# Three of the last gathers of a Trainium2 kernel split at token 120 into two gathers each

## The chip, the core and the metric

The kernel runs on one core of a Trainium2 chip. The metric is the device time of one execution in microseconds (us). The kernel before takes 1238.28 us, the median of 3 runs (1238.28 to 1238.28).

## The reference

Two blocks are computed on 256 tokens of width 1024 in fp32: a first block with a convolution branch, a differential attention and a cross attention, and a second block with a stick-breaking attention, a recurrent unit and, last, a PEER layer. The change lies in the PEER layer only:

```python
def chunk(xc):                                  # 128 tokens
    q = jnp.einsum('td,dhk->thk', xc, w_query)
    ...
    s = jnp.einsum('thpk,hpnk->thpn', q, sub_keys).astype(jnp.float32)
    top_s, top_i = lax.top_k(s, PEER_TOPK)
    ...
    idx = jnp.take_along_axis(cand_i, best_pos, axis=-1)
    g = jax.nn.softmax(best_s, axis=-1)
    u = jnp.take(expert_u, idx, axis=0)
    v = jnp.take(expert_v, idx, axis=0)
    act = jax.nn.gelu(jnp.einsum('td,thkd->thk', xc, u))
    return jnp.einsum('thk,thkd->td', (g * act).astype(v.dtype), v)
```

Each token picks 16 experts in each of 8 heads, 128 in all, out of 16384. An expert is a row u and a row v of 1024 fp32 numbers each. The token's output is the sum over its picks of a weight, times gelu(x . u), times v.

## The kernel before, in words

Up to about 590 us the kernel computes the first block and the mixing half of the second: weights are loaded piece by piece by SyncE (SP), each is split in two fp32r parts by ScalarE (ACT) and VectorE (DVE), and TensorE (PE) multiplies. From there to the end it works on the PEER layer, which is a loop over 256 picks, numbered g = 0 to 255. The tokens lie in two tiles t of 128, one token on a partition. Head by head and tile by tile (the list heads, 16 entries), each entry has 16 picks: picks 224 to 239 belong to entry 14, picks 240 to 255 to entry 15, both of tile 1.

For a pick g the four engines do this:

- **GpSimd (POOL)**, function gather (L2429 on): it waits until the expert's numbers are chosen ("picked") and until the buffer is free, and then issues one indirect DMA. It fetches for each of 128 tokens the 8 KB of its expert, u and v together, into a buffer of 128 x 2048 fp32 (1 MB). There are nine buffers in a ring (rows, UV): conv_in, three called big, four called row, and work_two. Gather g takes buffer g modulo 9, so it waits for PE to end pick g - 9. Each buffer has a semaphore of its own, gather0 to gather8.
- **DVE**, dot_product (L2062 in the profile): multiplies u with the tokens and sums, so it waits for the gather's semaphore. Then weigh (L2072) makes the coefficient.
- **ACT**, spread_value: the gelu (L1293), and then the coefficient on the diagonal of a 128 x 128 matrix (L1299).
- **PE**, add_value (L779): four matmuls of that diagonal with v, which add up in PSUM.

The order on DVE is dot_product(g + 1), weigh(g), and one step of choosing the experts of a later head: the steps of entry 14 start at pick 198, those of entry 15 at pick 214 (choose_at). Their end, which marks "picked", is L2034.

The last two picks, 254 and 255, are HALVED: u and v come by separate gathers of half rows (gather_half, L2440 on), both u first, then both v. The last v is not multiplied on PE but added by DVE (last_value, L2080); add_values (L2091) then adds PSUM to the residual, and SP and ACT write the halves of the output, SP at L2505, ACT at L1574. Tile 0's output is written earlier, some picks after pick 223.

SP has no work between its last weight load, at 577 us, and the output of tile 0.

The core of gather, which the change touches:

```python
e.indirect_dma_start(
    out=UV.ap(g), out_offset=None, in_=experts,
    in_offset=bass.IndirectOffsetOnAxis(ap=expert[t][:, n:n + 1], axis=0)
    ).then_inc(*mark(f"gather{g % len(rows)}", None, ("row", g), by=16))
```

Of the kernel before, what the change touches and what calls it, by code (L numbers as in the profile page):

```python
# [7 lines left out]
P = 128  # L8
F32 = mybir.dt.float32
F32R = mybir.dt.float32r  # L10
U32 = mybir.dt.uint32
# [29 lines left out]
PEER_TOPK = 16  # L41
# [21 lines left out]
class Marks:  # L63
# [13 lines left out]
    def mark(self, kind, key=None, *others, by=1):  # L77

        value = self.values[kind] = self.values.get(kind, 0) + by
        for name in (("#" + kind, value), (kind, key), *others):  # L80
            self.names[name] = kind, value
        return self.sem(kind), by
# [108 lines left out]
def build(nc, known, x, mem, vectors, weights, rg_w_a, rg_w_x, norm_ffn, sub_keys_t, experts,  # L191
          out):
    with ExitStack() as ctx:
        def sb(name, shape, dt=F32, space=ctx):
            return space.enter_context(nc.sbuf_tensor(name, [P, *shape], dt))

        def psum(name, n):
# [3 lines left out]
        mark, now, at = marks.mark, marks.now, marks.at  # L201
# [15 lines left out]
        ident, ones, ones64, later = (sb(n, [P]) for n in (  # L217
            "ident", "ones", "ones64", "later"))
# [1 line left out]
        ident_r, mask_r = (sb(n, [P], F32R) for n in ("ident_r", "mask_r"))  # L220
        iota16 = sb("iota16", [PEER_TOPK])
        col = sb("col", [144])
        sb("rows to 512 bytes", [96])

        def split_pair(space, name, columns):
            return [sb(f"{name}_{part}", [KT, columns], F32R, space) for part in ("hi", "lo")]
# [19 lines left out]
        def flat(ap):  # L246
            return ap.rearrange("p k t -> p (k t)")
# [79 lines left out]
        expert = [sel[:, t * 128:(t + 1) * 128].bitcast(U32) for t in range(TT)]  # L327
# [45 lines left out]
        for p in range(PIECES_ALL):  # L373
# [7 lines left out]
        rows = [sb(f"row{i}", [2 * D])[:, :] for i in range(4)]  # L381
        rows = [flat(conv_in[:, :, :])[:, 0:2 * D], big[2][:, :], big[0][:, :], big[1][:, :],
                *rows[2:], *rows[:2], work_two[:, :]]
# [4 lines left out]
        UV = Ring("uv", rows)  # L388
        diag_places = [probs.buffers[i % 2][:, i // 2 % 2, i // 4 * P:(i // 4 + 1) * P]
                       for i in range(12)]  # L390
        heads = [(t, h) for i in range(4) for t in range(TT) for h in (2 * i, 2 * i + 1)]
# [5 lines left out]
        for g in range(ALL_PICKS):  # L397
            UV.take(g)
        HALVED = (ALL_PICKS - 2, ALL_PICKS - 1)
        LAST = ALL_PICKS - 1  # L400
        final_sum = {t: max(g for g in range(LAST) if picks[g][0] == t) for t in range(TT)}
        half_rows = experts.rearrange("n (h d) -> (n h) d", h=2)
# [15 lines left out]
        def pe(e):  # L418
# [339 lines left out]
            def score(i, tiles=range(TT)):  # L758
                for t in tiles:
                    bank = banks.take(("score", i, t))  # L760
                    for wait in W(("queries", (i, t)), ("keys", None),
                                  banks.free(("score", i, t))):
                        e.wait_ge(*wait)
                    for j in range(4):
                        m = e.matmul(bank[:, j * P:(j + 1) * P],
                                     queries[:, j, t * P:(t + 1) * P], keys[:, 4 * i + j, :],
                                     start=True, stop=True)
                    m.then_inc(*mark("side_scores", (i, t), *([("scored", i)] if t else [])))

            def add_value(g):  # L770
                t, first = picks[g][0], g == first_pick[picks[g][0]]
                if first:
                    units.take(("y", t), t)
                unit = units.ap(("y", t))
                for wait in W(("diag", g), ("row", g) if g in HALVED else None,
                              units.free(("y", t)) if first else None):
                    e.wait_ge(*wait)
                for half in range(2):
                    m = e.matmul(unit[:, half * 512:(half + 1) * 512], diag_places[g % 12],  # L779
                                 UV.ap(g)[:, D + half * 512:D + (half + 1) * 512],  # L780
                                 start=first, stop=g == final_sum[t])
                    if half == 0 and g == final_sum[t]:
                        m.then_inc(*mark("added_half", t))
                m.then_inc(*mark("added", g, ("uv free", g)))
# [89 lines left out]
            score(0, [1])  # L874
            for g in range(LAST):
                add_value(g)
# [15 lines left out]
        def act(e):  # L892
# [394 lines left out]
            def spread_value(g):  # L1287
# [5 lines left out]
                e.activation(here, here, ACT.Gelu_apprx_tanh).then_inc(*mark("gelu", g))  # L1293
                if g == LAST:
                    return
# [283 lines left out]
        def dve(e):  # L1579
# [390 lines left out]
            def choose(head, eights=(0, 1)):  # L1970
# [68 lines left out]
                if head == len(heads) - 1:  # L2039
                    n = len(HALVED)  # L2040
                    e.scalar_tensor_tensor(out=row_f, in0=place_f[0][:, -n:],
# [15 lines left out]
            def dot_product(g):  # L2057
                t, n = picks[g]
                row_u = UV.ap(g)[:, 0:D]
                for wait in W(("row u" if g in HALVED else "row", g), ("h3", t)):  # L2060
                    e.wait_ge(*wait)
# [14 lines left out]
            def last_value():  # L2076
                t, n = picks[LAST]
                for wait in W(("coef", LAST), ("row", LAST)):
                    e.wait_ge(*wait)
                e.scalar_tensor_tensor(out=x_res[:, t, :], in0=UV.ap(LAST)[:, D:2 * D],  # L2080
                                       scalar=coef[t][:, n:n + 1], in1=x_res[:, t, :],
                                       op0=ALU.mult, op1=ALU.add).then_inc(*mark("last value"))
# [311 lines left out]
        def pool(e):  # L2394
            W = Reached(at)
# [33 lines left out]
            def gather(g):  # L2429
                t, n = picks[g]  # L2430
                for wait in W(("picked", g // PEER_TOPK, g % PEER_TOPK // 8),
                              UV.free(g) if g >= len(rows) else ROW_FREE[g]):
                    e.wait_ge(*wait)
                e.indirect_dma_start(  # L2434
                    out=UV.ap(g), out_offset=None, in_=experts,
                    in_offset=bass.IndirectOffsetOnAxis(ap=expert[t][:, n:n + 1], axis=0)
                    ).then_inc(*mark(f"gather{g % len(rows)}", None, ("row", g), by=16))

            def gather_half(g, half):
                i = HALVED.index(g)  # L2440
                for wait in W(("half rows", None), UV.free(g)):
                    e.wait_ge(*wait)
                e.indirect_dma_start(
                    out=UV.ap(g)[:, half * D:(half + 1) * D], out_offset=None, in_=half_rows,
                    in_offset=bass.IndirectOffsetOnAxis(ap=half_row[half][:, i:i + 1], axis=0)
                    ).then_inc(*(mark(f"gather{g % len(rows)}", None, ("row", g), by=16) if half
                                 else mark(f"gather u{i}", None, ("row u", g), by=16)))
# [13 lines left out]
            for c, base in ((slice(0, 256), -P), (slice(256, 384), 0)):  # L2461
                n = c.stop - c.start
# [12 lines left out]
            add_up("mix sB", P)  # L2475
            for g in range(HALVED[0]):
                gather(g)
            for half in range(2):
                for g in HALVED:
                    gather_half(g, half)  # L2480
# [3 lines left out]
        def sp(e):  # L2484
            W = Reached(at)
            for half in range(2):
                c = slice(half * SLOT, (half + 1) * SLOT)
                e.dma_start(x_tm[:, :, c], x_in[:, :, c]).then_inc(
                    *mark(f"load_x{half}", None, ("loaded", "x", half), by=16))
            for p in load_order:  # L2490
                place, prior = raw.place[p], raw.prior[p]
                for wait in W(RAW_FREE[p] if p in RAW_FREE else
                              None if prior is None else ("lo", prior)):
                    e.wait_ge(*wait)
                i = e.dma_start(flat(raw.ap(p)[:, :, :]), weights[p])
                i.then_inc(*mark(f"load_w{place}", p, ("loaded", p), by=16))
                if p == slot["pq0"].pieces[1]:
                    for wait in W(("scan", None)):
                        e.wait_ge(*wait)
                    e.dma_start(ffn_gain, norm_ffn).then_inc(  # L2500
                        *mark("load_gain", None, ("ffn gain", None), by=16))
            for t in range(TT):
                for wait in W(("y_out", (t, 0))):
                    e.wait_ge(*wait)
                e.dma_start(out_tm[:, t, 0:SLOT], x_res[:, t, 0:SLOT]).then_inc(  # L2505
                    *mark(f"out{t}0", by=16))
            for name in ("out00", "out10", "out01", "out11"):
                for wait in W((name, None)):
                    e.wait_ge(*wait)

        with nc.Block() as block:
            block.tensor(pe)
            block.scalar(act)
            block.vector(dve)
            block.gpsimd(pool)
            block.sync(sp)
# [66 lines left out]
```

## Time and profile before

| | us |
|---|---|
| median of 3 runs | 1238.28 |
| the profiled execution | 1239.19 |
| its span, first to last instruction | 1237.0 |
| PE busy | 1097.0 (89%) |
| DVE busy | 979.1 (79%) |
| POOL busy | 590.0 (48%) |
| ACT busy | 549.7 (44%) |

The profiled execution is 0.91 us above the median, and 2.2 us of it lie outside the span. Engine names: PE TensorE, PEld its weight loads, DVE VectorE, ACT ScalarE, POOL GpSimd, SP SyncE; a q behind a name (POOLq, SPq) is the engine's own instruction queue, from which DMAs are issued. A timeline row gives the start in us, the duration in us, the engine, the line, the operation, out<-in, and in brackets the engine's idle time before it and what ended that. In the rows of GB/s a stretch is cut in 40 equal slices. The core has 16 DMA engines, and every digit of a DMA row is their mean busy share in tenths.

### The profile page before, as it was taken

What the parts mean: (1) busy time and instruction counts of PE and PEld (TensorE: products, weight loads), DVE (VectorE), ACT (ScalarE), POOL (GpSimd) and SP (SyncE); (2) the same over time, 40 slices, a digit from 0 to 9 for tenths busy, and PEclk for the clock granted to TensorE, in tenths of its full rate; (3) what the DMA queues carried; (4) which work ended last, traced back from release to release, by engine and by line L of the source; (5) the groups of instructions that cost most, each with busy time, mean ns of one, the idle gap of its engine ahead of it and who ended that gap; (6) DMA issues with size and microseconds to landing.
All of it is one profiled execution on the core that took longest, in us unless ns stands there. A gap on an engine that the chain in (4) does not pass through costs nothing.

```text
span 1237.0 us, 13575 instructions
## 1 busy us (share of the span) xinstructions
PE 1097.0 (89%) x4676; PEld 724.1 (59%) x4676; DVE 979.1 (79%) x1960; ACT 549.7 (44%) x1070; POOL 590.0 (48%) x547
## 2 busy tenths in 40 slices
PE   6999999999999999999588887888879888787877
PEld 6988888788989889977244433444324443222322
DVE  6599999998887767686988777887778867877655
ACT  5665676654456444994433233323332233222311
POOL 0089999999840000010554545553545545444432
PEclk9999999999999999999799999999999999999999
DMA  6554434444464655336899999999999999999996
GB/s 248 193 182 170 171 137 139 155 149 165 176 214 160 225 188 179 132 137 255 358 427 426 428 427 428 426 427 426 426 427 427 427 427 427 427 427 410 427 427 275
DMA packets 53941, 374.23 MB, mean 303 GB/s; under 512 B 6896, under 2 KB 6896, under 8 KB 9200
## 3 DMA queue, kind: packets, MB, share of 16 engines
q0 software_dynamic: 37152, 268.45, 51.6%
q1 hardware_dynamic: 14512, 100.67, 22.8%
q10 hardware_dynamic: 2208, 4.24, 1.0%
q8 instruction: 37, 0.61, 0.2%
q14 instruction: 32, 0.26, 0.1%
HBM read 372.29 MB, written 1.05 MB: 302 GB/s over the span
## 4 chain that ended last, share of the span: by engine, by line
PE 44%; DMA 25%; DVE 24%; ACT 4%; issue 3%; POOL 0%; POOLq 0%; DVEq 0%; SPq 0%; ACTq 0%
DMA big<-in_experts,big 11%; PE unit L450 10%; PE unit L452 10%; PE unit L451 10%; PE unit L779 9%; DMA row<-in_experts,big 6%; DMA conv_in<-in_experts,big 4%; DVE w_lo L1589 3%; DVE row L2062 3%; DMA work_two<-in_experts,big 2%; DVE big L2062 2%; DVE big L1968 2%; DVE conv_acc L1612 2%; DVE big L1965 2%; DVE big L2072 1%
## 5 line engine op out<-in xcount | busy, mean ns | idle before, releaser
L1299 ACT ACTIVATE probs<-ident,big 128x128 f32<-128x128 f32 x255 | 102.4, 402 | 430.8 <-DVE big L2072 430.8
L779 PE MATMUL unit<-row,probs 128*128 128x512 f32 x448 | 215.4, 610 | 45.9 <-ACT probs L1299 45.7
L1589 DVE TENSOR_TENSOR w_lo<-w_raw,w_hi 128x2048 fp32r<-128x2048 f32 x89 | 207.6, 2339 | 50.3 <-ACT w_hi L907 50.3
L907 ACT CAST w_hi<-w_raw 128x2048 fp32r<-128x2048 f32 x89 | 169.4, 1905 | 87.3 <-DMA w_raw<-in_weights 45.8
L779 PE MATMUL unit<-big,probs 128*128 128x512 f32 x344 | 168.3, 620 | 39.3 <-ACT probs L1299 39.2
L2434 POOL DMA_INDIRECT row<-in_experts,big x112 | 134.2, 1198 | 128.6 <-PE unit L779 112.1
L450 PE MATMUL unit<-in_hi,w_hi 128*128 128x256 f32 x544 | 189.2, 348 | 1.6 <-DVE in_lo L1676 0.9
L450 PE MATMUL unit<-w_hi,in_hi 128*128 128x512 f32 x432 | 171.0, 396 | 0.7 <-ACT big L1044 0.7
L779 PEld LDWEIGHTS unit<-row,probs 128*128 128x128 f32 x448 | 78.3, 190 | 156.1 <-ACT probs L1299 97.2
L451 PE MATMUL unit<-w_hi,in_lo 128*128 128x512 f32 x432 | 168.3, 390 | 0.0
L452 PE MATMUL unit<-w_lo,in_hi 128*128 128x512 f32 x432 | 168.3, 390 | 0.0
L2062 DVE CUSTOM_DVE_ANT_0 row<-big,row 128x1024 f32<-128x1024 f32 x112 | 136.6, 1220 | 37.7 <-DMA row<-in_experts,big 37.6
L2434 POOL DMA_INDIRECT big<-in_experts,big x85 | 102.7, 1208 | 118.3 <-PE unit L779 104.3
L451 PE MATMUL unit<-in_lo,w_hi 128*128 128x256 f32 x544 | 153.7, 283 | 0.0
L452 PE MATMUL unit<-in_hi,w_lo 128*128 128x256 f32 x544 | 153.6, 282 | 0.0
L2415 POOL TENSOR_TENSOR conv_acc<-conv_acc,big 128x256 f32<-128x256 f32 x132 | 140.6, 1065 | 11.0
L2411 POOL TENSOR_SCALAR big<-conv_in,early_small 128x256 f32<-128x256 f32 x132 | 136.6, 1035 | 3.5 <-DVE conv_acc L1612 2.5
L779 PEld LDWEIGHTS unit<-big,probs 128*128 128x128 f32 x344 | 61.3, 194 | 127.7 <-ACT probs L1299 80.2
L2062 DVE CUSTOM_DVE_ANT_0 big<-big 128x1024 f32<-128x1024 f32 x87 | 106.1, 1219 | 34.3 <-DMA big<-in_experts,big 34.3
L450 PEld LDWEIGHTS unit<-in_hi,w_hi 128*128 128x128 f32 x544 | 104.2, 191 | 23.0 <-issue 20.5
L451 PEld LDWEIGHTS unit<-in_lo,w_hi 128*128 128x128 f32 x544 | 104.1, 191 | 20.5 <-issue 20.3
L452 PEld LDWEIGHTS unit<-in_hi,w_lo 128*128 128x128 f32 x544 | 104.0, 191 | 0.0
(319 smaller groups left out, 1672.0 us busy)
## 6 DMA issues: line engine op xcount, KB each, us to landing
w_raw<-in_weights SPq DMA_DIRECT2D x90, 1024.0 KB, 4.8
w_waiting<-in_weights SPq DMA_DIRECT2D x2, 1024.0 KB, 9.1
row<-in_experts,big POOLq DMA_INDIRECT x112, 14.8
big<-in_experts,big POOLq DMA_INDIRECT x89, 13.4
big<-in_x SPq DMA_DIRECT2D x2, 512.0 KB, 5.1
big<-in_mem ACTq DMA_DIRECT2D x1, 1024.0 KB, 4.9
big<-in_x ACTq DMA_DIRECT2D x1, 1024.0 KB, 6.6
big<-in_sub_keys_t ACTq DMA_DIRECT2D x1, 1024.0 KB, 6.8
```

The source lines that it names most:

```text
L450: e.matmul(unit[:, to], *hi_hi, start=first, stop=False)
L451: e.matmul(unit[:, to], *hi_lo, start=False, stop=False)
L452: m = e.matmul(unit[:, to], *lo_hi, start=False, stop=final)
L779: m = e.matmul(unit[:, half * 512:(half + 1) * 512], diag_places[g % 12], UV.ap(g)[:, D + half * 512:D + (half + 1) * 512], start=first, s ...
L907: e.copy(split.ap(p)[0][:, :, :], raw.ap(p)[:, :, :]).then_inc(*mark("hi", p))
L1299: e.activation(diag_places[g % 12], ident[:, :], ACT.Copy, scale=here).then_inc(*mark("diag", g))
L1589: e.tensor_tensor(lo_part[:, :, :], raw.ap(p)[:, :, :], hi_part[:, :, :].bitcast(F32), ALU.subtract).then_inc(*mark("lo", p))
L1612: i = e.scalar_tensor_tensor(out=dst, in0=src, scalar=tap, in1=dst, op0=ALU.mult, op1=ALU.add)
L2062: e.tensor_tensor_reduce(out=row_u, in0=h3[:, t, :], in1=row_u, scale=1.0, scalar=0.0, op0=ALU.mult, op1=ALU.add, accum_out=dot[t][:, n:n ...
L2411: e.tensor_scalar(product, src, tap, 1.0, ALU.mult, ALU.mult).then_inc(*mark("pool_product", (t, k)))
L2415: e.tensor_tensor(dst, dst, product, ALU.add).then_inc(*mark("pool_tap", None, *done))
L2434: e.indirect_dma_start(out=UV.ap(g), out_offset=None, in_=experts, in_offset=bass.IndirectOffsetOnAxis(ap=expert[t][:, n:n + 1], axis=0)). ...
```

## The change

Gathers 226, 231 and 236 (entry 14, picks 2, 7 and 12 of its sixteen) are issued as two indirect DMAs into the same buffer: one for tokens 0 to 119, and one for tokens 120 to 127. An indirect DMA of 8 tokens takes its expert numbers from the first 8 partitions here, so SP copies the numbers of tokens 120 to 127 of all sixteen picks of entry 14 (8 x 16 words) to a new tile, later_part_expert, on partitions 0 to 7. POOL waits for that copy between the first part and the second part of gather 226. Both parts add 16 to the buffer's semaphore, and a reader waits for both. The new tile takes 16 of the 96 columns of a filler, so no other address moves.

```diff
+        later_part_expert = sb("later_part_expert", [PEER_TOPK], U32)
-        sb("rows to 512 bytes", [96])
+        sb("rows to 512 bytes", [80])
...
+        PARTED_HEAD, FIRST_PART = len(heads) - 2, 120
+        PARTED = [PARTED_HEAD * PEER_TOPK + j for j in (2, 7, 12)]
...
+                if g in PARTED:
+                    j, n_part = g % PEER_TOPK, P - FIRST_PART
+                    e.indirect_dma_start(
+                        out=UV.ap(g)[0:FIRST_PART, :], out_offset=None, in_=experts,
+                        in_offset=bass.IndirectOffsetOnAxis(
+                            ap=expert[t][0:FIRST_PART, n:n + 1], axis=0)
+                        ).then_inc(*mark(f"gather{g % len(rows)}", by=16))
+                    for wait in W(("later part", None)):
+                        e.wait_ge(*wait)
+                    e.indirect_dma_start(
+                        out=UV.ap(g)[FIRST_PART:P, :], out_offset=None, in_=experts,
+                        in_offset=bass.IndirectOffsetOnAxis(
+                            ap=later_part_expert[0:n_part, j:j + 1], axis=0)
+                        ).then_inc(*mark(f"gather{g % len(rows)}", None, ("row", g), by=16))
+                    return
...
+            t, h = heads[PARTED_HEAD]
+            for wait in W(("picked", PARTED_HEAD, 0), ("picked", PARTED_HEAD, 1)):
+                e.wait_ge(*wait)
+            e.dma_start(later_part_expert[0:P - FIRST_PART, :],
+                        expert[t][FIRST_PART:P, h * PEER_TOPK:(h + 1) * PEER_TOPK]).then_inc(
+                *mark("later_part", None, ("later part", None), by=16))
```

On POOL, the gathers 224 to 238 stand in this row before (an entry with x3 or x4 is so many gathers into buffers of that name; the first row is gather 224, and "choose" is its wait for the picks of entry 14):

```order
L2434 DMA work_two<-in_experts,big 128x2048 [waits added,choose]
L2434 DMA conv_in<-in_experts,big 128x2048 [waits added]
L2434 DMA big<-in_experts,big 128x2048 [waits added] x3
L2434 DMA row<-in_experts,big 128x2048 [waits added] x4
L2434 DMA work_two<-in_experts,big 128x2048 [waits added]
L2434 DMA conv_in<-in_experts,big 128x2048 [waits added]
L2434 DMA big<-in_experts,big 128x2048 [waits added] x3
```

And with the change, from the same gather on:

```order
L2452 DMA work_two<-in_experts,big 128x2048 [waits added,choose]
L2452 DMA conv_in<-in_experts,big 128x2048 [waits added]
L2439 DMA big<-in_experts,big 120x2048 [waits added]
L2446 DMA big<-in_experts,later_part_expert 8x2048 [waits later_part]
L2452 DMA big<-in_experts,big 128x2048 [waits added] x2
L2452 DMA row<-in_experts,big 128x2048 [waits added] x2
L2439 DMA row<-in_experts,big 120x2048 [waits added]
L2446 DMA row<-in_experts,later_part_expert 8x2048
L2452 DMA row<-in_experts,big 128x2048 [waits added]
L2452 DMA work_two<-in_experts,big 128x2048 [waits added]
L2452 DMA conv_in<-in_experts,big 128x2048 [waits added]
L2452 DMA big<-in_experts,big 128x2048 [waits added]
```

Behind this, gather 236 is parted in the same way. Three issues more stand on POOL, one wait more at the first of them, and nothing has changed places.

On SP, the end of the queue (the last weight load, then the copy, then the outputs) reads so with the change:

```order
L2513 DMA w_waiting<-in_weights 128x2048 [waits piece]
L2513 DMA w_waiting<-in_weights 128x2048
L2513 DMA w_raw<-in_weights 128x2048 [waits lo]
L2523 DMA later_part_expert<-big 8x16 [waits choose]
L2529 DMA out_x<-big 128x512 [waits y_out] x2
```

The copy is new, and the two output DMAs of SP stand behind it and its wait. PE, DVE and ACT have the same rows in the same order as before.

## Rows read from the trace of the kernel before

**Rows 1.** The page: the span, the 40 slices of 30.9 us, and the queues
```profile
span 1237.0 us, 13575 instructions
DMA  6554434444464655336899999999999999999996
GB/s 248 193 182 170 171 137 139 155 149 165 176 214 160 225 188 179 132 137 255 358 427 426 428 427 428 426 427 426 426 427 427 427 427 427 427 427 410 427 427 275
q0 software_dynamic: 37152, 268.45, 51.6%
```

**Rows 2.** Busy time by stretches of the PEER loop and of its end
```profile
core 0: us, PE busy (x) PEld busy (x) DVE busy (x) ACT busy (x) POOL busy (x), PEclk, DMA share, GB/s
1144.00:1205.00 61.00, 48.79 (x98) 17.74 (x99) 37.05 (x90) 15.45 (x54) 26.22 (x25) 0.97 1.01 427
1222.00:1223.00 1.00, 1.00 (x3) 0.19 (x1) 1.00 (x3) 0.00 (x0) 0.00 (x0) 1.00 1.03 410
1224.00:1225.00 1.00, 1.00 (x3) 0.38 (x2) 0.74 (x1) 0.00 (x0) 0.00 (x0) 1.00 0.54 221
1225.00:1226.00 1.00, 0.65 (x2) 0.00 (x0) 0.63 (x3) 0.34 (x2) 0.00 (x0) 1.00 0.18 74
1226.00:1227.00 1.00, 0.88 (x2) 0.49 (x3) 0.49 (x2) 0.56 (x3) 0.00 (x0) 1.00 0.07 29
1230.00:1231.00 1.00, 1.00 (x3) 0.50 (x4) 0.61 (x3) 0.36 (x2) 0.00 (x0) 1.00 0.06 25
```

**Rows 3.** The DMA view of 1226 to 1232 us, in slices of 0.15 us
```profile
GB/s 55 0 27 27 27 27 27 27 27 27 27 27 27 27 27 27 0 27 27 27 27 27 27 27 27 27 27 27 27 27 27 27 27 27 27 0 0 0 0 0
DMA packets 38, 0.14 MB, mean 23 GB/s; under 512 B 5, under 2 KB 5, under 8 KB 37
```

**Rows 4.** Timeline of DVE, its last two rows
```profile
1231.76 1.28 DVE L2080 SCALAR_TENSOR_TENSOR big<-big 128x1024 f32<-128x1024 f32 x1 [0.37 <-DMA big<-in_experts,big]
1233.15 1.29 DVE L2091 TENSOR_TENSOR big<-unit,big 128x512 f32<-128x512 f32 x2
```

**Rows 5.** Timeline of DVE at four picks from 1202 us on
```profile
1202.33 1.23 DVE L2062 CUSTOM_DVE_ANT_0 conv_in<-big,conv_in 128x1024 f32<-128x1024 f32 x1 [2.05 <-DMA conv_in<-in_experts,big]
1203.48 0.22 DVE L2072 SCALAR_TENSOR_TENSOR big<-big 128x1 f32<-128x1 f32 x1
1204.76 1.23 DVE L2062 CUSTOM_DVE_ANT_0 big<-big 128x1024 f32<-128x1024 f32 x1 [1.06 <-DMA big<-in_experts,big]
1207.19 1.23 DVE L2062 CUSTOM_DVE_ANT_0 big<-big 128x1024 f32<-128x1024 f32 x1 [1.07 <-DMA big<-in_experts,big]
```

**Rows 6.** Gathers (L2434) of two stretches, issue to landing: 620 to 720, 1150 to 1205 us
```profile
DMA to landing us min/median/max: 9.3/11.7/12.9
...
DMA to landing us min/median/max: 15.5/16.1/16.4
```

**Rows 7.** Timeline of PE at the end: one pick in steady state, the last two
```profile
1221.22 1.99 PE L779 MATMUL unit<-row,probs 128*128 128x512 f32 x4 [0.46 <-ACT probs L1299]
1229.82 3.70 PE L779 MATMUL unit<-big,probs 128*128 128x512 f32 x8
```

**Rows 8.** Timeline of POOL: gathers 226, 227; 231, 232; 236 to 238
```profile
1142.98 1.55 POOL L2434 DMA_INDIRECT big<-in_experts,big  x1 [0.78 <-PE unit L779]
1146.61 1.69 POOL L2434 DMA_INDIRECT big<-in_experts,big  x1 [2.08 <-PE unit L779]
...
1155.11 0.94 POOL L2434 DMA_INDIRECT row<-in_experts,big  x1 [1.52 <-PE unit L779]
1157.59 0.94 POOL L2434 DMA_INDIRECT row<-in_experts,big  x1 [1.53 <-PE unit L779]
...
1168.35 1.86 POOL L2434 DMA_INDIRECT big<-in_experts,big  x1 [0.56 <-PE unit L779]
1170.51 0.94 POOL L2434 DMA_INDIRECT big<-in_experts,big  x1 [0.30 <-issue]
1172.28 0.94 POOL L2434 DMA_INDIRECT row<-in_experts,big  x1 [0.83 <-PE unit L779]
```

**Rows 9.** End of choosing entry 14 on DVE; SP's outputs, and out_x to landing
```profile
1119.86 0.17 DVE L2034 SCALAR_TENSOR_TENSOR big<-big 128x16 uint32<-128x16 f32 x1
...
1165.28 68.93 SPq L2505 DMA_DIRECT2D out_x<-big  x2
...
DMA to landing us min/median/max: 2.0/2.0/7.0
```

## The prediction

> **What bounds the kernel now.** I read the page first. The second half of the span is a DMA stage: from slice 20 (about 620 us) on, the DMA row shows nines and the rate stands at 427 GB/s [rows 1]. That is 1.05 MB every 2.45 us, one gather, and the picks indeed follow each other on DVE in 2.43 us, each waiting about 1.07 us for its gather's landing, not for another engine [rows 5]. PE (48.79 of 61.00 us), DVE (37.05) and POOL (26.22) all have room in the stage [rows 2]. So the loop goes at the pace at which gathers land.
>
> A gather has landed when the last of 16 DMA engines is through. The queue row gives 37152 packets for 258 gathers (254 whole ones and four of half rows), which is 144 for each, or 9 for each DMA engine [rows 1]: eight rows of 8 KB and one packet that signals, if the rows are dealt out evenly. Full rate is then 427 / 16 = 26.7 GB/s for one DMA engine.
>
> Next I looked at the end of the gathers in short stretches. The rate is 410 GB/s up to 1223 us, 221 in the microsecond from 1224, 74 in that from 1225, and then 25 to 29 until 1231 [rows 2]. In slices of 0.15 us it is 27 GB/s, slice after slice, without a gap that matters, for 5 us [rows 3]. This is the rate of exactly one DMA engine. **Fifteen have finished by about 1226.1 us, and one works on alone until 1231.3 us.** DVE waits for it: the last value's instruction starts at 1231.76 us with 0.37 us of wait for the DMA, and only that multiplication, the two additions and the output stand behind it [rows 4].
>
> How late is that one? From 1226.1 us to the landing at 1231.7 us it is 5.6 us; by its bytes, 33 packets of 4 KB after 1226 us (38 less 5 small ones) [rows 3], 33 x 4096 B / 26.7 GB/s = 5.1 us. I take 5.5. The lag was gathered along the way: the time from issue to landing has a median of 11.7 us early in the stage and of 16.1 us late in it, though the issue always waits for the buffer of nine picks before [rows 6]. Single steps can be seen, such as a wait of 2.05 us at a pick where it is 1.06 at its neighbours, 1.0 us lost [rows 5]. A busy DMA engine never makes such a step good, since it has the same eight rows a gather as all the others.
>
> **The change part by part.**
>
> *The first part, 120 tokens.* At eight rows for each DMA engine, 120 rows occupy fifteen and leave one out. If the one left out is the late one, it saves 8 rows x 8192 B / 26.7 GB/s = 2.45 us at each of gathers 226, 231 and 236.
>
> *The second part, 8 tokens.* One row each on eight DMA engines costs those 0.31 us a gather, 0.92 us over three. If the late one is not among them it saves 3 x 2.45 = 7.4 us in all, if it is, 6.4 us. Both are more than 5.5 us, so it stops being the last, and the other fifteen set the end. Some of these are now later by 0.92 us. By the slope of the rate (74 GB/s in the microsecond from 1225, some three at work) [rows 2] the last few of the fifteen end within about 1 us of each other, and eight of fifteen get the extra rows. So the gain at the end is between 5.5 - 0.92 = 4.6 us (the very last gets them) and 5.6 us (none near the end does). I take 4.8 us, since one of the last two or three most likely has them.
>
> *Can the engines follow?* The picks have to come closer together for a while. PE is the narrowest: 8 matmuls in 3.70 us, 1.85 us a pick, against the 2.44 it now has with 0.46 idle [rows 7]. DVE needs 1.23 + 0.22 us and some 0.1 for reading the sum [rows 5]. 2.45 - 1.85 is 0.6 us gained back a pick, so 4.8 us take 8 picks; between gather 236 and the end there are 19. Cost: nothing. After the last landing the same 5.3 us (1231.7 to 1237.0) follow.
>
> *POOL.* Three more issues of 0.94 us and about 0.3 us between two, 1.24 us each; an issue has been as long as 1.86 us [rows 8], which bounds it at 2.2. Behind gather 226 the next starts 3.63 us later, having waited 2.08 us for PE, and behind 231 it starts 2.48 us later with 1.53 of wait, so both cover it. Behind 236 POOL is short: 237 follows with only 0.30 us of idle, and is pushed back 1.24 us; 238 had waited 0.83 us and is pushed back 0.4 us, and then it is gone [rows 8]. The cover is the stock of issued gathers: 16.1 us from issue to landing [rows 6], less the lag of 5.5 and the transfer of 2.45, leaves some 8 us of queue ahead of even the fast DMA engines. Cost: nothing. Without that stock it would be 1.24 us three times, 3.7 us.
>
> *SP's copy and the new wait.* The experts of entry 14 are chosen at 1120.0 us, and gather 226 is issued at 1142.98 us [rows 8, 9]. There are 23 us for a copy of 512 B; the nearest rows are the outputs of 256 KB, which land 2.0 to 7.0 us after issue [rows 9]. So POOL's new wait is at an end before it is reached. Behind the copy SP holds only the outputs, the first of them at 1165.28 us [rows 9], 45 us later. Cost: nothing, and 512 B are no load.
>
> **Sum.** Against the profiled execution, 1239.19 - 4.8 = 1234.4 us. That execution is 0.91 us above the median of the runs, so against the median 1238.28 - 4.8 = **1233.5 us**.
>
> **The rivals.**
>
> *The relief hits another DMA engine.* No row says which tokens the late one carries. If it is not the one left out, it is as late as before, and with an extra row in each second part 0.92 us later: 1238.3 to 1239.2 us. In favour is only that the trace gives no name; against it, that the late one has been hit by steps of its own all along, which points to something fixed about it. The Trainium skill, DMA: Bandwidth & Descriptors, section Latency and other measured facts, says that of the sixteen the engines 7 and 15 are usually the slower ones in traces. By that rule the late one is 7 or 15, and only 15 is the one left out by a split at 120; were it 7, the sum would be the 0.92 us of loss instead of the 4.8 us of gain. The trace agrees that one lags, by 5.5 us, and does not name it. Chance 0.13.
>
> *The place left out moves on.* If a gather that uses fewer than sixteen DMA engines starts where the one before it stopped, then the first part of 226 leaves out the last, and those of 231 and 236 others. The late one saves 8 rows once and pays one row twice: 2.45 - 0.61 = 1.8 us, 1236.4 us. Nothing in the trace speaks to it, since every gather there has 128 tokens. The same page of the Trainium skill, section Why a DMA increments its semaphore by 16 and not by 1, states such a moving start for transfers on fewer than 16 engines, and an exception for some direct copies, which stay on the first ones; by the moving start this rival's time is the result, by the exception the forecast's. Chance 0.11.
>
> *Slower: 120 rows go to eight DMA engines.* If the rows are dealt in a way that wants a power of two, each of eight gets fifteen rows, seven more than now, and with the second part one more: 3 x 8 x 0.307 = 7.4 us on the same eight. Is the late one among them, then 1238.3 + 7.4 = 1245.7 us; if not, the others overtake it, 7.4 - 5.5 = 1.9 us, 1240.2 us. It decides from about 18 extra rows on, where 18 x 0.307 equals the lag. Against it: 120 divides by 15. Chance 0.03, and 0.02 for a stall of POOL that drains the stock (up to 3.7 us, 1242).
>
> *Relief with a leak.* The relief works, but the pace or the stock costs 1 to 2 us of it, 1235 to 1236 us. Chance 0.04.
>
> **How the numbers follow.** The forecast has 0.67. A measurement of this kernel can tell a change from none by about 0.2%, 2.5 us. Faster by more than that are the forecast and the leak: 0.71. Within it are the wrong engine and the moving place: 0.24. Slower: 0.05. The range begins at 1232.0, below 1238.3 - 5.6 = 1232.7 us by the spread of single executions; upward it takes in the leak and the moving place and ends at 1237.0 us. Outside are the wrong engine and the slower cases, 0.18.
>
> **What would show it.** In the profile after, the stretch at 25 to 29 GB/s at the end of the gathers should be gone or under 1 us, with full rate up to some 1224 us and DVE's last value at about 1227 us. From issue to landing it should fall from 16 us to 11 or 12 us by gather 240, in three steps near 226, 231 and 236, after which PE shows less idle time for some picks. If the tail of one engine's rate stays 5 us long, the wrong one was relieved; if 3 to 4 us are left, the place moves; a tail of eight engines' rate (213 GB/s) means the slower rival. A wait of POOL at the second part of 226 would prove the copy late. The forecast is wrong if the tail goes and the time does not: then PE held the end.

## The result, and the profile after

The changed kernel takes 1258.08 us (median of 5 runs, 1255.97 to 1259.92) against 1238.28 us (5 runs, 1237.67 to 1238.28): **19.8 us slower**, a ratio of 1.0159 with the interval 1.0148 to 1.0171. The prediction was 1233.5 us with a range up to 1237.0. The profiled execution of the change took 1259.92 us, with a span of 1258.2.

The page of the changed kernel, span and slices (31.5 us each), and the queue of the gathers:

```profile
span 1258.2 us, 13579 instructions
DMA  7445443444463655445999999999999999999996
GB/s 273 174 171 186 153 158 134 140 162 162 173 234 139 230 176 182 154 184 217 425 427 426 427 427 427 427 426 427 427 428 426 426 427 426 426 427 351 277 370 245
q0 software_dynamic: 37248, 268.45, 52.3%
```

In the gather stage nothing has changed against [rows 1] up to slice 35, about 1133 us: 425 to 428 GB/s. Then three slices follow at 351, 277 and 370 GB/s, and the DMA engines' busy share stays at nines. The same stretches, cut finer:

```profile
core 0: us, PE busy (x) PEld busy (x) DVE busy (x) ACT busy (x) POOL busy (x), PEclk, DMA share, GB/s
1100.00:1140.00 40.00, 30.48 (x64) 10.82 (x63) 29.85 (x88) 10.99 (x36) 18.92 (x16) 1.00 1.01 427
1140.00:1150.00 10.00, 7.91 (x18) 2.99 (x18) 8.47 (x26) 1.98 (x8) 6.96 (x6) 1.00 1.02 367
1150.00:1160.00 10.00, 6.02 (x10) 2.04 (x9) 3.55 (x9) 1.70 (x4) 2.55 (x4) 0.83 1.01 283
1160.00:1170.00 10.00, 5.18 (x11) 1.54 (x9) 4.16 (x13) 3.36 (x9) 4.15 (x4) 1.00 1.04 273
1180.00:1190.00 10.00, 5.69 (x12) 1.77 (x11) 2.88 (x7) 1.10 (x4) 2.58 (x3) 1.00 1.05 254
```

This pair of columns is the finding: a DMA share of 1.01 to 1.05, and 254 to 283 GB/s where it was 427 in [rows 2]. The DMA engines are not starved and not idle. They are all at work, and each packet takes longer. The durations of the single packets in the two traces say the same: before, 3104 of the 3110 packets of 8 KB between 1144 and 1205 us took 0.32 us or less (median 0.309), and in the change, between 1148 and 1156 us, one of 209 did (median 0.60). From 1140 to 1210 us the seven stretches of 10 us show 367, 283, 273, 322, 254, 342 and 378 GB/s, 770 GB/s short of seven times 427. That is 770 x 10 / 427 = 18.0 us of full rate, most of the loss. From 1210 to 1240 us the rate is 372 GB/s at a busy share of 0.95, which is another 30 x 55 / 427 = 3.9 us, in part with engines idle. The two together, 21.9 us, are close to the 20.7 us between the two profiled executions.

Timeline of DVE in the first dip (picks 222 to 226 of the changed kernel, the dot products alone; 225 is left out):

```profile
1147.69 1.27 DVE L2065 CUSTOM_DVE_ANT_0 row<-big,row 128x1024 f32<-128x1024 f32 x1 [0.79 <-DMA row<-in_experts,big]
1152.59 1.23 DVE L2065 CUSTOM_DVE_ANT_0 row<-big,row 128x1024 f32<-128x1024 f32 x1 [3.16 <-DMA row<-in_experts,big]
1157.38 1.23 DVE L2065 CUSTOM_DVE_ANT_0 work_two<-big,work_two 128x1024 f32<-128x1024 f32 x1 [3.08 <-DMA work_two<-in_experts,big]
...
1165.03 1.23 DVE L2065 CUSTOM_DVE_ANT_0 big<-big 128x1024 f32<-128x1024 f32 x1 [2.04 <-DMA big<-in_experts,later_part_expert]
```

Where the wait for a landing was 1.06 us [rows 5], it is now 3 us, and at whole gathers of earlier picks (the rows called row and work_two, picks 223 and 224) before the parted one is read at 1165 us. The parted gather slows what is still on its way when it starts.

The copy and the issues behave as forecast. SP copies at 1119.22 us, and POOL issues both parts of gather 226 without a wait for it, and so it goes at the other two:

```profile
1142.19 1.57 POOL L2439 DMA_INDIRECT big<-in_experts,big  x1 [0.81 <-PE unit L782]
1144.06 1.52 POOL L2446 DMA_INDIRECT big<-in_experts,later_part_expert  x1 [0.30 <-issue]
1145.88 1.39 POOL L2452 DMA_INDIRECT big<-in_experts,big  x1 [0.30 <-PE unit L782]
```

And the end of the gathers, in stretches of 2 us:

```profile
1244.00:1246.00 2.00, 1.55 (x4) 0.67 (x4) 0.91 (x4) 0.49 (x2) 0.00 (x0) 1.00 0.53 215
1246.00:1248.00 2.00, 1.53 (x4) 0.46 (x4) 1.11 (x5) 0.86 (x3) 0.00 (x0) 1.00 0.06 27
1250.00:1252.00 2.00, 1.98 (x6) 0.67 (x5) 1.82 (x6) 0.65 (x3) 0.00 (x0) 1.00 0.07 27
```

One DMA engine again works alone at 27 GB/s from 1246 us to past 1252, no shorter than in [rows 2, 3]: by the packets of the traces it is alone for 6.8 us here and for 5.6 us before. The late engine was not relieved.

### The profile page after: what moved, and what is told of

Read it like the earlier page. It is cut to its first block, busy times and chain, and to the rows that moved or that the text cites. A ratio compares the mean times of both kernels' runs of the same rounds, so it can differ in the third digit from the quotient of the medians.

```text
span 1258.2 us, 13579 instructions
## 1 busy us (share of the span) xinstructions
PE 1098.8 (87%) x4676; PEld 723.1 (57%) x4676; DVE 979.1 (78%) x1960; ACT 549.9 (44%) x1070; POOL 595.8 (47%) x550
## 3 DMA queue, kind: packets, MB, share of 16 engines
q1 hardware_dynamic: 14528, 100.67, 21.9%
HBM read 372.29 MB, written 1.05 MB: 297 GB/s over the span
## 4 chain that ended last, share of the span: by engine, by line
PE 48%; DMA 25%; DVE 19%; ACT 4%; issue 3%; POOL 0%; POOLq 0%; DVEq 0%; SPq 0%; ACTq 0%
PE unit L453 11%; PE unit L455 11%; PE unit L454 11%; DMA big<-in_experts,big 11%; PE unit L782 9%; DMA row<-in_experts,big 8%; DMA conv_in<-in_experts,big 4%; DVE row L2065 3%; DMA work_two<-in_experts,big 2%; DVE big L1971 2%; DVE big L2065 2%; DVE w_lo L1592 2%; DVE big L1968 2%; DVE conv_acc L1615 1%; DVE big L2075 1%
## 5 line engine op out<-in xcount | busy, mean ns | idle before, releaser
L2452 POOL DMA_INDIRECT row<-in_experts,big x111 | 136.1, 1226 | 134.9 <-PE unit L782 119.0
L2065 DVE CUSTOM_DVE_ANT_0 row<-big,row 128x1024 f32<-128x1024 f32 x112 | 136.6, 1220 | 46.6 <-DMA row<-in_experts,big 43.0
L2452 POOL DMA_INDIRECT big<-in_experts,big x83 | 98.0, 1181 | 120.1 <-PE unit L782 106.1
L2065 DVE CUSTOM_DVE_ANT_0 big<-big 128x1024 f32<-128x1024 f32 x87 | 106.1, 1220 | 42.7 <-DMA big<-in_experts,big 37.1
L453 PEld LDWEIGHTS unit<-in_hi,w_hi 128*128 128x128 f32 x544 | 104.5, 192 | 21.4 <-issue 20.7
```

What stands on the lines that cost most here:

```text
L453: e.matmul(unit[:, to], *hi_hi, start=first, stop=False)
L2065: e.tensor_tensor_reduce(out=row_u, in0=h3[:, t, :], in1=row_u, scale=1.0, scalar=0.0, op0=ALU.mult, op1=ALU.add, accum_out=dot[t][:, n:n ...
L2452: e.indirect_dma_start(out=UV.ap(g), out_offset=None, in_=experts, in_offset=bass.IndirectOffsetOnAxis(ap=expert[t][:, n:n + 1], axis=0)). ...
```

## The experiments

Each ratio is to runs of the kernel before that were made together with the variant (median 1238.0 to 1238.5 us). A variant's time less that median is its loss.

**Which part costs.** Three kernels: the 120-token gathers alone, the 8-token gathers alone, the copy alone. The second:

```diff
                     e.indirect_dma_start(
-                        out=UV.ap(g)[0:FIRST_PART, :], out_offset=None, in_=experts,
+                        out=UV.ap(g), out_offset=None, in_=experts,
...
-                            ap=expert[t][0:FIRST_PART, n:n + 1], axis=0)
+                            ap=expert[t][:, n:n + 1], axis=0)
...
-                        out=UV.ap(g)[FIRST_PART:P, :], out_offset=None, in_=experts,
+                        out=extra_rows[PARTED.index(g)][FIRST_PART:P, :], out_offset=None, in_=experts,
```

Here the gathers are whole and the 8-token gather goes into a buffer that nobody reads. The first kernel drops the second indirect_dma_start, so it leaves out tokens 120 to 127 of three picks; the third keeps only SP's copy and POOL's wait.

> What it leaves out: the gathers of tokens 120 to 127 at picks 226, 231 and 236 (those eight tokens use what the buffer held before). The gathers of tokens 0 to 119, the copy and the wait stay. Theory A, the 120-token gather itself is moved at half rate and holds up the others (in the profile of the change the DMA rate falls to about 213 GB/s while the DMA engines stay fully busy): nearly all of the loss stays, 1254 to 1258 us, with dips to half rate behind each of the three. Theory B, the 8-token gather is what costs (few engines, descriptors in another order): the loss goes and the time is 1233 to 1239 us. Theory C, the copy and the wait: as theory A in time, but then the run with the copy alone shows it too.

> The three gathers are whole (128 tokens) again, and the 8-token gather follows each of them, into a buffer that nobody reads, with the same wait for the copy. It computes the same output with 24 rows of 8 KB more. Theory A (the 120-token gather costs): 1238 to 1240 us, the added rows being 0.3 us each on eight engines. Theory B (the 8-token gather costs): 1250 us or more, with dips to half rate. A little of both: in between, and the two runs then add up to the change's 19.8 us.

> The copy by SyncE and the wait on GpSimd alone, no gather is parted. Theories A and B: 1238.3 us within 0.5. Theory C, the copy or the wait costs: near 1258 us. The profile of the change shows the copy issued at 1119 us and no wait for it on GpSimd, which speaks against C.

Measured: 120 tokens alone 1257.12 us (ratio 1.0153, 1.0136 to 1.0169), 8 tokens alone 1239.83 us (1.0014, 1.0004 to 1.0024), the copy alone 1238.41 us (1.0002, 0.9993 to 1.0012). The 120-token gathers carry 19.1 of the 19.8 us, the small ones 1.8 when they stand alone, and the copy and the wait nothing. Theory A holds: it is the 120-token gather that costs. In the kernel with the 120-token gathers alone the rate dips in the same places:

```profile
1150.00:1160.00 10.00, 4.84 (x11) 1.81 (x10) 3.90 (x9) 2.21 (x5) 2.85 (x3) 0.98 1.01 270
1160.00:1170.00 10.00, 7.66 (x11) 2.23 (x11) 4.47 (x15) 3.34 (x10) 3.17 (x3) 0.68 1.04 306
1180.00:1190.00 10.00, 4.79 (x10) 1.84 (x11) 2.73 (x6) 1.50 (x6) 2.85 (x3) 1.00 1.03 258
```

**One parted gather, and where it stands.** Gather 226 alone (`for j in (2,)`), then one alone at pick 28 (PARTED_HEAD 1, j 12), then one alone at pick 253 (PARTED_HEAD 15, j 13).

> Only gather 226 is parted (120 and 8). If each parted gather costs by itself: a third of 19.8 us, 1244 to 1246 us. If the late DMA engine is the one that the split at 120 relieves, part of the cost comes back at the end. If the three together do it (one puts the engines out of step, the next finds them so): less than a third, under 1242 us; or, if the first one already puts them out of step for good, nearly all of it, above 1250 us.

> One gather alone is parted (120 and 8), but early: pick 28 instead of 226. At pick 28 the DMA engines are nearly in step (the late one has not fallen back yet). If the cost of one parted gather (8.0 us at pick 226) comes from its meeting with gathers of other picks, because the late engine is two gathers behind: 2.5 to 4 us here, 1241 to 1242 us. If it is a property of the gather alone: 8 us again, 1246 us. A stall of GpSimd for the copy is possible here and would be seen as a wait.

> One gather is parted (120 and 8), the last whole one, pick 253. The fast DMA engines have nothing but four half gathers behind it. If the cost is that of DMA engines that are out of step and get in each other's way for several gathers, less is left to be held up: 1239 to 1242 us, below the 8.0 us of the split at pick 226. If the late engine were relieved by a split at 120 at all (2.45 us), then the time would be at or below 1238.3 us, as hardly anything stands against it here. If the gather costs the same anywhere: 1246 us.

Measured: pick 226 1246.07 us (1.0066, 1.0049 to 1.0083), 8.0 us; pick 28 1242.18 us (1.0032, 1.0022 to 1.0042), 3.7 us; pick 253 1243.22 us (1.0041, 1.0026 to 1.0056), 5.2 us. The first is at the upper end of what was expected, the second 0.2 us and the third 1.2 us above it. So each parted gather costs by itself (three together cost 6.6 us each), and the cost depends on where it stands. With pick 226 parted, the DMA view of 1140 to 1200 us in slices of 1.5 us:

```profile
GB/s 431 410 426 437 251 197 142 164 218 235 208 300 431 382 377 355 388 404 426 410 431 382 404 392 421 433 431 426 403 430 423 431 431 431 426 426 421 415 421 426
```

With pick 28 parted, stretches of 10 us:

```profile
650.00:660.00 10.00, 5.95 (x12) 2.03 (x12) 9.73 (x31) 1.90 (x8) 4.65 (x5) 1.00 1.01 426
660.00:670.00 10.00, 9.38 (x32) 5.17 (x33) 8.71 (x28) 2.06 (x9) 3.87 (x5) 1.00 1.02 248
670.00:680.00 10.00, 8.78 (x31) 4.69 (x29) 6.83 (x17) 4.99 (x12) 4.39 (x5) 1.00 1.01 426
```

Early in the stage there is one dip, (427 - 248) x 10 / 427 = 4.2 us, and it is over in 10 us. At pick 226 there are 12 us of dip, down to 142 GB/s, and a second, shallow one behind it. This is what was expected if a gather disturbs those it meets and meets more of them when the DMA engines are far out of step. The two cases differ in other ways too, though (PE's other work at pick 28), so the size of that share is argued, not isolated.

**Uneven work, or the way in which rows are dealt out.** The split moved from 120 to other tokens:

```diff
-        PARTED_HEAD, FIRST_PART = len(heads) - 2, 120
+        PARTED_HEAD, FIRST_PART = len(heads) - 2, 126
```

and the same with 112 and with 64.

> The three gathers are split at token 126 (126 and 2 tokens). Theory D, what costs is how the rows of a gather of other than 128 tokens are dealt out: DMA engines write into partitions that others write at the same time, two share one way in and each goes at half rate. Then 126 is as bad as 120: 1255 to 1260 us with the DMA rate near 213 GB/s behind each. Theory E, what costs is that work is uneven, with one DMA engine left out: with eight rows on fifteen of them and six on the last it is nearly even again, and the time is 1238 to 1241 us. If the number of engines used is the largest divisor (14 for 126, nine rows each), theory E gives 1 row more on each of 14, about 1239 us, and D remains slow.

> The three gathers are split at token 112 (112 and 16). Both numbers are multiples of 16, so each of the 16 DMA engines gets seven rows and one row: perfectly even. Theory E (uneven work): 1238 to 1241 us. Theory D (rows dealt so that engines write where others write): still slow, 1250 to 1262 us, with dips of the rate.

> The three gathers are split in the middle (64 and 64), four rows and four rows for each DMA engine. Theory E: 1238 to 1240 us. Theory D: in a gather of 64 tokens all sixteen engines write into half of the partitions; if the way in is per group of partitions, only half of the ways are used at a time, the rate is near 213 GB/s for 2.1 MB or more in all, and the loss is at least 3 x 2.45 = 7.4 us, 1245 us or more.

Measured: 126 and 2 tokens 1257.05 us (1.0144, 1.0127 to 1.0161); 112 and 16 tokens 1254.75 us (1.0138, 1.0122 to 1.0155); 64 and 64 tokens 1257.94 us (1.0155, 1.0138 to 1.0172). The losses are 18.6, 16.3 and 19.5 us, against 19.8 with the split at 120, so all are nearly as slow. With 112 and 16, and with 64 and 64, both gathers divide by sixteen and the work is even, so uneven work is not the cause. In the DMA view of the split in the middle (1140 to 1200 us) the dips lie near one value:

```profile
DMA  9999999999899999999999999999999999999999
GB/s 415 431 415 415 431 339 197 235 235 213 218 399 415 410 382 366 300 180 246 218 224 218 213 328 437 431 375 407 332 197 208 191 208 235 251 351 395 434 431 415
```

213 to 218 GB/s is half of 427, with all engines busy. What is shown: a gather of 120 tokens among gathers of 128 makes the packets take about twice as long for some 10 us, and so do the pairs of 126 and 2, 112 and 16, and 64 and 64 tokens; in the kernel before, with gathers of 128 tokens, 30965 of 31059 packets of 8 KB between 620 and 1220 us took 0.32 us or less. Of the pairs only the 120-token gather was also run alone. Why is argued: with 128 tokens each DMA engine would write into partitions of its own, with fewer the rows would be dealt out otherwise, so that two engines write into the same group of partitions. The kernel before reads the same experts' rows at full rate, which speaks against the reading side, though no run separates reading from writing. The Trainium skill, DMA: Bandwidth & Descriptors, section The descriptor swizzle, gives just such an assignment of engines to partition groups for 128 partitions, one port each, and says nothing of the rate at other sizes. The rates here agree with it, but they don't prove it: the trace does not list the partitions of a packet.

**Which DMA engine is late.** Small gathers of 8 and 7 tokens into unread buffers behind each of the gathers 226 to 239 (with `extra_rows` as above and EXTRA = 8 or 7):

> No gather is parted. Each of the gathers 226 to 239 (14) is followed by one more of 8 tokens into buffers that nobody reads, on partitions 64 to 119 only. It measures which DMA engines a small gather uses: one row on each of the first eight, it is thought. If the late engine is among those eight, it gets 14 rows more, 14 x 0.31 = 4.3 us, 1242.5 us or a little more. If it is not, the others eat into its lag of 5.5 us and the time stays at 1238 to 1240 us.

> The same with 7 tokens each, so one DMA engine fewer gets a row. If the late engine is the eighth one (number 7), it has no extra row here: 1238 to 1240 us, and 3 to 4 us less than with 8 tokens. If it is one of the first seven: as with 8 tokens. If it is the sixteenth (15), which the split at 120 would relieve: both runs near 1238 to 1240 us.

Measured: 1248.83 us (1.0088, 1.007 to 1.0106) and 1246.4 us (1.007, 1.0052 to 1.0088), both above every expectation, so they give no answer. POOL in the kernel with 7 tokens, and the stretch from 1160 to 1170 us:

```profile
1161.32 0.88 POOL L2453 DMA_INDIRECT w_raw<-in_experts,later_part_expert  x1 [0.30 <-issue]
1162.49 1.40 POOL L2446 DMA_INDIRECT work_two<-in_experts,big  x1 [0.30 <-issue]
1164.20 0.87 POOL L2453 DMA_INDIRECT w_raw<-in_experts,later_part_expert  x1 [0.30 <-issue]
1165.38 0.97 POOL L2446 DMA_INDIRECT conv_in<-in_experts,big  x1 [0.31 <-issue]
```

```profile
1160.00:1170.00 10.00, 5.96 (x13) 2.03 (x12) 6.13 (x19) 1.72 (x7) 7.87 (x8) 1.00 1.00 344
```

POOL issues without a pause, 2.9 us for two issues where a pick has 2.45. But it is not what binds: the DMA engines are fully busy (share 1.00 to 1.02) at 332 to 363 GB/s from 1150 to 1190 us in both kernels, so the small gathers too make packets take longer. To take POOL out of the question all the same, the small gathers were spread, one behind every third gather from 160 to 240, onto partitions from 64 or from 96 on:

```diff
-        PARTED_HEAD, FIRST_PART = len(heads) - 2, 120
-        PARTED = [PARTED_HEAD * PEER_TOPK + j for j in (2, 7, 12)]
+        PARTED_HEAD, FIRST_PART = 8, 112
+        PARTED = list(range(160, 241, 3))
```

> All gathers are whole. Behind every third gather from 160 to 240 (27 in all) one more gather of 7 tokens follows, into buffers that nobody reads, one row each on seven DMA engines. GpSimd has time for it (one issue more in three picks), unlike in the two runs with 14 in a row. If the late DMA engine is not among the seven: 1238 to 1240 us. If it is: 27 x 0.31 = 8.3 us more, 1246 us or above.

> The same with 8 tokens each. If the late engine is the eighth one, the whole 8.3 us appear between 7 and 8 tokens: 1246 us or above here, near 1239 us with 7. If it is the sixteenth, or any other of the upper eight: 1238 to 1241 us with 7 and with 8, since the other engines have 5.5 us of lead and lose 8.3 us of it, at most 3 us show.

> The same with 16 tokens each, one row on every DMA engine: the late one gets 27 rows more wherever it is, 8.3 us, 1246 to 1248 us. It is the measure for the other two: the one with 7 or 8 tokens that comes close to it has the late engine among its engines.

Measured: 7 tokens 1263.16 us (1.0198, 1.0181 to 1.0215), 8 tokens 1268.95 us (1.0245, 1.0228 to 1.0262), 16 tokens 1282.35 us (1.035, 1.0332 to 1.0367). All lie far above the 1238 to 1248 us that the price of a row gave: 25.0, 30.8 and 44.2 us for 27 small gathers are 0.93, 1.14 and 1.64 us each, where their bytes at 427 GB/s are 0.13, 0.15 and 0.31 us. Again with busy engines; 8 tokens:

```profile
1000.00:1100.00 100.00, 74.30 (x170) 29.52 (x171) 65.82 (x188) 26.31 (x84) 50.94 (x47) 0.97 1.01 391
1100.00:1200.00 100.00, 69.22 (x139) 23.88 (x137) 64.78 (x186) 22.99 (x76) 48.94 (x46) 0.98 1.00 370
```

Not every packet is slow here: with 8 tokens, between 1100 and 1200 us, 81% of the packets of 8 KB still took 0.32 us or less, while the slowest took 1.98 us. It looks as if something is crowded that only some of the engines share at a time. The cost with 8 tokens is near that of four rows one after another, 4 x 0.307 = 1.2 us, which would be the price of neighbouring tokens' rows going into one group of four partitions; that is argued too, and the same count gives 1.2 us for 7 and for 16 tokens, where 0.93 and 1.64 were measured.

The times don't tell the late engine then, but the signals in the trace do tell something. The last signal of a small gather and the last of the whole gather ahead of it come from the engine that is late. Their distance is 0.3 us or more where that engine has a row in between, as with 16 tokens, when every engine has one (0.30 to 0.88 us, all 27 times), and 0.17 to 0.19 us where it has none. Read this way, the runs say three things.

First, the small gathers make another engine the late one. With 16 tokens the late engine is 2.6 us behind the next at pick 160, 0.4 us at pick 184, and then the lead grows again, to 10.2 us at pick 235: it has been overtaken. With 7 and with 8 tokens the same happens around pick 180. So what the runs show behind that pick is not the late engine of the kernel before.

Second, **the place where a small gather starts moves on.** With 8 tokens, from pick 196 on, the distance is 0.17 to 0.18 us at every second small gather and 0.52 to 0.74 us at those between (217 falls out with 5.4 us, where one signal is missing from the trace). With 7 tokens the fifteen distances from pick 196 on (seven of 0.30 to 0.63 us, eight of 0.17 to 0.18 us) come in just the order that a start moving on by seven of sixteen engines gives, for one place of the engine alone, the ninth counted from the start of the first small gather.

Third, the late engine of the kernel before has its place as well. With 7 tokens the distances at picks 160 to 178 are 0.72, 0.18, 0.69, 0.19, 0.18, 0.63 and 0.19 us. This order comes out only for the fourth or the fifth engine from the first start. In the change, if 120 tokens take fifteen engines and 8 tokens eight, and each part starts where the one before it stopped, from that same first start, the first parts leave out the sixteenth engine at gather 226, the seventh at 231 and the fourteenth at 236, so the late one never. This is worked out, not seen, but the signals of the change agree with it: from the gather before to the first part of each parted gather it takes 4.9, 4.6 and 4.6 us in place of 2.45, so the late one had its eight rows, at half rate, every time. (The distance to the second part's signal, 0.28, 0.33 and 0.33 us, doesn't tell whether it had a row there too.) Which number the engine has stays open, as no run shows at which engine the first small gather starts.

No arrangement tried is faster than the kernel before; every one with a gather of other than 128 tokens cost time. A version that takes rows from the late engine and leaves the rest in gathers of 128 tokens was not tried.

## Why the prediction was wrong

- **What bounds the kernel** was right. The loop goes at the pace of landings, one DMA engine is 5.5 us behind, and the stage's time follows the rate: the loss can be read off the dips. (Of the 38 packets in [rows 3], 32 are of 4 KB and one is larger, where 33 were counted; it makes 5.2 us of the 5.1.)
- **The step that failed is the first part, 120 tokens.** Its rows were priced at 0.307 us, from gathers of 128 tokens, for that gather and all others around it. That is the price of a row only while all gathers have the same form. No row of the trace showed a gather of another number of tokens, so the price had nothing behind it for this part and for its neighbours, and the working doesn't say so. The runs showed packets that take twice as long on all engines for some 10 us: 19.1 us for the three first parts alone, 6.4 each, in place of a gain. Why the packets slow down is argued above, not shown.
- **The relief** (2.45 us three times) measured nothing: the tail of one engine at 27 GB/s is no shorter than before (6.8 against 5.6 us). The rival of the moving place had it right in kind: the start moves on, and by the order of the signals the engine left out was never the late one, so the forecast's gain would have been missing without the slow packets too. That rival still gave it one relief of 2.45 us. By the Trainium skill's rule of the moving start, which the prediction cites from DMA: Bandwidth & Descriptors, section Why a DMA increments its semaphore by 16 and not by 1, its 1236.4 us would have come out; the trace agrees with the rule for gathers of 7 and of 8 tokens, and the slow packets, which the rule doesn't speak of, decided the time. The same page's remark on engines 7 and 15 is neither borne out nor refuted, since no run names the late engine.
- **The second part** was put at 0.31 us a gather; alone it measured 1.8 us for three, 0.6 each, and 1.14 us each in the run with 27.
- **POOL, SP's copy, the new wait:** right. The copy and the wait alone measure 1238.41 us, and POOL's extra issues let no engine run dry: the busy share is 0.99 or more from 1140 to 1210 us.
- **PE follows:** not tested by the change, as the landings never came closer together.
- **The slower rival** had the sign and not the mechanism: a tail of eight engines was expected, with some idle, and the rows show all sixteen busy at half rate. The 0.05 for any slower result was too low. The only thing set against that rival was that 120 divides by 15, which says how many engines work, and nothing of how they share the way into memory.

## What to carry to other kernels

In a stream of equal DMAs that keeps all engines busy, the time of a row is a price for that stream only, and not for a DMA of another shape: measure one odd DMA in the stream before moving bytes between engines. Look at busy share and GB/s together; here busy engines at half rate meant that packets took twice as long, while idle ones would have meant that issue or work was missing. And a lag of one engine of sixteen is worth at most its tail (5.5 us here), whereas what slows all sixteen costs the whole stream.

## What was not expected of the hardware

- A gather of 128 rows of 8 KB that is split into 64 and 64, 112 and 16, 120 and 8 or 126 and 2, in a stream of whole ones, costs 5.4 to 6.6 us (three of each: 16.3 to 19.8 us), though it moves no byte more; the rate falls from 427 to 213 GB/s or below (142 in one slice of 1.5 us) with a busy share of 1.0, and the median packet of 8 KB takes 0.60 us in place of 0.309.
- Even small gathers of 7, 8 or 16 tokens cost 0.93, 1.14 and 1.64 us each in such a stream.
- The queue's packets: 27 small gathers add 864 packets, 32 each, with 7, 8 and 16 tokens alike (38016 in all three runs against 37152). So each of the 16 DMA engines gets two packets; where it has no row, a packet of 4 B stands in the row's place (25, 24 and 16 packets of 4 B a small gather, for 7, 8 and 16 tokens).
- A small gather of 8 tokens gives the same DMA engine a row only every second time, and with 7 tokens the order fits a start that moves on by seven engines each time.
